# TensorE's rounds of attention work in another order, in a two-layer encoder on one core

## The reference, cut to what matters

```
proj = x @ w_in + b_in          # q_a k_a v_a g_a | q_b k_b v_b g_b | q_idx k_idx w_idx | r_a r_b
# index scores, top-k: which keys a query may see in branch B
index_score = sum_h w_idx[h] * relu(q_idx[h] . k_idx)
# branch B: softmax attention over the selected keys (8 heads, one shared key/value)
p = softmax(q_b k_b * scale + bias, selected keys only);   y_b = p v_b
# branch A: stick-breaking attention (8 heads)
z = q_a k_a * scale;  log_keep = log_sigmoid(-z) for keys before the query
later = sum of log_keep over the later keys before the query
y_a = exp(log_sigmoid(z) + later) v_a
merged = sigmoid(r_a) * ((y_a * silu(g_a)) @ w_proj_a) + sigmoid(r_b) * ((y_b * silu(g_b)) @ w_proj_b)
x = layer_norm(ALPHA * x + merged @ w_out)
```

## Time and profile before

| | us |
|---|---|
| median of 3 runs | 1096.7 (1094.59 to 1096.8) |
| the profiled execution, its own time | 1093.59 |
| its span, first to last instruction | 1091.8 |
| PE busy | 1040.2 (95%) |
| DVE busy | 566.0 (52%) |
| POOL busy | 492.9 (45%) |
| ACT busy | 474.6 (43%) |

### The profile page before, as it was taken

How to read it: one execution, slowest core, us unless ns; L and a number is a source line. 1 busy time by engine, 2 the same in 40 slices (tenths; PEclk the granted TensorE clock), 3 DMA queues, 4 the chain that set the end, 5 groups by cost and what they waited for, 6 DMA issues and landing times.

```text
span 1091.8 us, 18589 instructions
## 1 busy us (share of the span) xinstructions
PE 1040.2 (95%) x7557; PEld 921.0 (84%) x7557; DVE 566.0 (52%) x1163; ACT 474.6 (43%) x812; POOL 492.9 (45%) x334
## 2 busy tenths in 40 slices
PE   1899999998999999999999999999899999999997
PEld 1877898776889999998788599977688999999975
DVE  7438997777773111101580699877777331101137
ACT  2244335667774432223223533476777462222310
POOL 3222355453554745445434244554445474444550
PEclk9999999999999999999999999999999999999999
DMA  6621443011111223423225223321101222242322
GB/s 198 210 78 50 147 149 131 2 40 40 40 40 63 76 90 113 143 77 117 89 79 186 62 72 101 98 83 41 40 5 36 78 78 78 78 174 85 110 76 86
DMA packets 70457, 96.61 MB, mean 88 GB/s; under 512 B 4587, under 2 KB 61381, under 8 KB 69733
## 3 DMA queue, kind: packets, MB, share of 16 engines
q1 hardware_dynamic: 66068, 82.68, 23.1%
q0 software_dynamic: 3872, 11.64, 3.3%
q10 hardware_dynamic: 432, 1.11, 0.3%
HBM read 79.46 MB, written 14.78 MB: 86 GB/s over the span
## 4 chain that ended last, share of the span: by engine, by line
PE 83%; DVE 6%; ACT 3%; POOL 3%; DMA 2%; issue 2%; SPq 0%; DVEq 0%; ACTq 0%
PE ps L503 43%; PE ps L821 10%; PE ps L780 7%; PE ps L695 5%; PE ps L604 3%; PE ps L588 2%; PE ps L646 2%; PE ps L657 2%; PE ps L674 2%; DMA raw<-in_w_in 2%; POOL w_lo L1454 1%; DVE x_nat L1178 1%; PE ps L755 1%; PE ps L734 1%; PE ps L712 1%
## 5 line engine op out<-in xcount | busy, mean ns | idle before, releaser
L1454 POOL TENSOR_TENSOR w_lo<-raw,w_hi 128x1024 fp32r<-128x1024 f32 (+1 forms) x116 | 282.0, 2432 | 374.9 <-ACT w_hi L872 374.8
L503 PE MATMUL ps<-xT_hi,w_hi 128*128 128x288 f32 x960 | 284.9, 297 | 2.8 <-POOL w_lo L1454 2.8
L503 PE MATMUL ps<-xT_hi,w_lo 128*128 128x288 f32 x960 | 282.8, 295 | 0.0
L503 PE MATMUL ps<-xT_lo,w_hi 128*128 128x288 f32 x960 | 282.7, 294 | 0.0
L503 PEld LDWEIGHTS ps<-xT_hi,w_hi 128*128 128x128 f32 x960 | 180.1, 188 | 4.8 <-POOL w_lo L1454 3.4
L503 PEld LDWEIGHTS ps<-xT_lo,w_hi 128*128 128x128 f32 x960 | 180.1, 188 | 0.0
L503 PEld LDWEIGHTS ps<-xT_hi,w_lo 128*128 128x128 f32 x960 | 180.1, 188 | 0.0
L872 ACT ACTIVATE w_hi<-raw 128x1024 fp32r<-128x1024 f32 (+1 forms) x116 | 121.0, 1045 | 122.1 <-PE ps L503 72.7
L1415 DVE TENSOR_TENSOR qy<-qy,ps 128x576 f32<-128x576 f32 x32 | 24.1, 754 | 253.8 <-PE ps L503 253.8
L921 ACT ACTIVATE qy<-ps,bias 128x576 f32<-128x576 f32 x40 | 29.7, 743 | 151.6 <-PE ps L503 148.6
L1546 POOL TENSOR_TENSOR attn<-attn 128x1024 f32<-128x1024 f32 (+1 forms) x24 | 55.2, 2298 | 71.5 <-DVE attn L1350 71.5
(11 more groups left out here) (173 smaller groups left out, 2144.3 us busy)
## 6 DMA issues: line engine op xcount, KB each, us to landing
raw<-in_w_in SPq DMA_DIRECT2D x44, 1024.0 KB, 5.2
raw<-in_w_out SPq DMA_DIRECT2D x8, 1024.0 KB, 5.0
x_kept<-x_nat SPq DMA_DIRECT2D x2, 2560.0 KB, 11.6
x_nat<-x_kept SPq DMA_DIRECT2D x2, 2560.0 KB, 11.6
raw<-in_w_proj_a SPq DMA_DIRECT2D x8, 512.0 KB, 3.5
raw<-in_w_proj_b SPq DMA_DIRECT2D x8, 512.0 KB, 4.5
x_nat<-in_x_prompt SPq DMA_DIRECT2D x4, 512.0 KB, 8.5
out<-stage POOLq DMA_DIRECT2D x8, 256.0 KB, 4.9
```

The lines of the kernel that those rows point to most:

```text
L503: last = mm(out, a, b[:, HALF * half:HALF * (half + 1)], start=(k == 0 and i == 0), stop=(k == n - 1 and i == 2))
L1454: g.tensor_tensor(lo, src, hi.bitcast(f32), ALU.subtract).then_inc(s_lo, 1)
```

## The change

- Softmax: round p has L, V(p-4), T(p-2), D in place of L, T(p-2), V(p-3), D. The first two Z stand at the head of their rounds.
- Between the loops: two dense halves in place of one; the last V of softmax goes into the first round of stick-breaking.
- Stick-breaking: round p has Z(p), V(p-4), T(p-3), D in place of T(p-3), Z(p), D, V(p-3); the halves of the gates come one round earlier. In chunk 2 the sample's two products come ahead of the prompt's.
- Index scores: two pairs ahead of every 12 dense matmuls in place of one ahead of every 6.
- DVE: in softmax `yb_out` stands between the two `masked_logits`; in stick-breaking `sum_later` comes a round later, and `mask_z` waits for the transposes only ahead of its second output. ACT: one `head` moves ahead of the loop. POOL: the `rest` of a gate unit follows an earlier `log_weight`.

```diff
-HALVES_AT = {p: [p - 2] if p < NP else [2 * p - 14, 2 * p - 13] for p in range(A_LAG, NP + A_LAG)}
+HALVES_AT = {p: [p - 1] for p in range(A_LAG - 1, NP)} | {NP: [11, 12], NP + 1: [13, 14], NP + 2: [15]}
@@ dense_with_scores
-                            if k % 2 == 0:
+                            if k % 4 == 0:
                                 index_scores(s + 8 * half + k)
+                                index_scores(s + 8 * half + k + 2)
@@ stick_z: the products of c == 2 with q_s (L716) now stand ahead of the loop over A_TILES[c] (L712)
@@ PE, softmax
-                for p in range(NBP + 3):
+                for p in range(NBP + 2):
                     if p < NBP:
                         logits(p)
+                    else:
+                        stick_z(p - NBP)
+                    if p >= 4:
+                        weigh_values(p - 4)
                     if p == 2:
                         pe.wait_ge(s_trev, L * N_TR + N_TR)
-                    if 2 <= p < NBP + 2:
+                    if p >= 2:
                         transpose_probs(2 * p - 4)
                         transpose_probs(2 * p - 3)
-                    if NBP <= p < NBP + 2:
-                        stick_z(p - NBP)
-                    if p >= 3:
-                        weigh_values(p - 3)
                     if p < len(QA_GROUPS):
                         qa_group(*QA_GROUPS[p])
                 stick_z(2)
+                weigh_values(NBP - 2)
                 dense_half(0)
+                dense_half(1)
@@ PE, stick-breaking
                 for p in range(A_LAG, NP + A_LAG):
-                    stick_transpose(p - A_LAG)
                     if p < NP:
                         stick_z(p)
+                    if p == A_LAG:
+                        weigh_values(NBP - 1)
+                    else:
+                        stick_values(p - A_LAG - 1)
+                    stick_transpose(p - A_LAG)
                     for n in HALVES_AT[p]:
                         dense_half(n)
-                    stick_values(p - A_LAG)
+                stick_values(NP - 1)
@@ ACT, after log_term(2)
+                head(N_G + 2)
@@ DVE, mask_z: the wait for s_at (transposes of p - 3) now stands behind the writes of sp_slot
@@ DVE, softmax and after
-                for p in range(NBP + 4):
+                for p in range(NBP):
+                    masked_logits(2 * p)
                     if p >= 4:
                         yb_out(p - 4)
-                    if p < NBP:
-                        masked_logits(2 * p)
-                        masked_logits(2 * p + 1)
-                    if 1 <= p < NBP + 1:
+                    masked_logits(2 * p + 1)
+                    if p >= 1:
                         normalise(p - 1)
-                    (p == NBP: mask_z(0); NBP + 1: mask_z(1); NBP + 2: sum_later(0))
+                yb_out(NBP - 4)
+                normalise(NBP - 1)
+                mask_z(0)
+                yb_out(NBP - 3)
+                mask_z(1)
+                sum_later(0)
                 mask_z(2)
+                yb_out(NBP - 2)
                 sum_later(1)
                 gate_half(0)
-                sum_later(2)
                 for p in range(A_LAG, NP + A_LAG + 1):
+                    if p < NP:
+                        mask_z(p)
+                    if p == A_LAG:
+                        yb_out(NBP - 1)
+                    for n in HALVES_AT[p - 1]:
+                        gate_half(n)
                     if p > A_LAG and (p - A_LAG) % A_CHUNKS == 0:
                         ya_out((p - A_LAG) // A_CHUNKS - 1)
-                    (mask_z(p), gate_half of HALVES_AT[p], sum_later(p))
+                    if p <= NP:
+                        sum_later(p - 1)
@@ POOL, after log_weight(p)
-                    if p >= A_LAG:
-                        for n in HALVES_AT[p]:
-                            if n % 2:
-                                rest(N_G + 2 + n // 2)
-                for n in range(5, A_UNITS):
+                    for n in HALVES_AT.get(p + 1, []):
+                        if n % 2:
+                            rest(N_G + 2 + n // 2)
+                for n in range(6, A_UNITS):
                     rest(N_G + 2 + n)
```

More of the change, by code:

```diff
@@ L708, in stick_z @@
                         pe.wait_ge(s_zm, L * NP + p)
+                    if c == 2:
+                        for n in range(2):
+                            mm(ps[:, n, 256:256 + S_HALF], q_s[:, m, :, :],
+                                      kT_a[:, m, S_HALF * n:S_HALF * n + S_HALF], start=True, stop=True)
                     for i, at, nk in A_TILES[c]:
@@ L713, in stick_z @@
                                       kT_a[half, m, PAST + DEC:PAST + DEC + nk], start=True, stop=True)
[L714 to L717, removed]
                     last.then_inc(s_z, 1)
@@ L1316, in mask_z @@
                     if p >= 3:
-                        dve.wait_ge(s_at, L * NP + p - 2)
+                        dve.wait_ge(s_lw, L * NP + p - 2)
                     elif p:
                         dve.wait_ge(s_pt, L * N_B + N_B)
-                    if p >= 3:
-                        dve.wait_ge(s_lw, L * NP + p - 2)
                     n = 256 if c == 2 else 512
@@ L1335, in mask_z @@
                                            ALU.add).then_inc(s_min, 1)
+                    if p >= 3:
+                        dve.wait_ge(s_at, L * NP + p - 2)
                     if c == 2:
@@ L1371, in ya_out @@
                     v.tensor_copy(qy[:, 4 + m, DEC:TOK], ps[:, 6, :]).then_inc(s_ya, 1)
-                for p in range(NBP + 4):
+                for p in range(NBP):
+                    masked_logits(2 * p)
                     if p >= 4:
                         yb_out(p - 4)
-                    if p < NBP:
-                        masked_logits(2 * p)
-                        masked_logits(2 * p + 1)
-                    if 1 <= p < NBP + 1:
+                    masked_logits(2 * p + 1)
+                    if p >= 1:
                         normalise(p - 1)
[L1381 to L1386, removed]
+                yb_out(NBP - 4)
[4 more added lines that the diff above has]
+                sum_later(0)
                 mask_z(2)
+                yb_out(NBP - 2)
                 sum_later(1)
                 gate_half(0)
-                sum_later(2)
                 for p in range(A_LAG, NP + A_LAG + 1):
+                    if p < NP:
[4 more added lines that the diff above has]
+                        gate_half(n)
                     if p > A_LAG and (p - A_LAG) % A_CHUNKS == 0:
                         ya_out((p - A_LAG) // A_CHUNKS - 1)
-                    if p < NP:
-                        mask_z(p)
-                    if p < NP + A_LAG:
-                        for n in HALVES_AT[p]:
-                            gate_half(n)
-                    if p < NP:
-                        sum_later(p)
+                    if p <= NP:
+                        sum_later(p - 1)
                 dve.wait_ge(s_ya, L * 2 * PAIRS + 2 * PAIRS)
```

## The result

| | before | after |
|---|---|---|
| median | 1095.64 us (1093.96 to 1096.8, 4 runs) | 1070.99 us (1070.61 to 1071.31, 4 runs) |
| profiled execution, its own time | 1093.59 | 1071.31 |
| its span | 1091.8 | 1069.5 |

What follows compares the result with a forecast made beforehand. PE, busy 95% of the span, was taken as the bound. Per layer 2.4 + 3.2 + 3.7 + 1.4 + 1.2 = 11.9, twice 23.8, off 1093.6: 1069.8; plus 3.1, 1072.9, said as 1072; 8-of-10 range 1066 to 1083.

Steps and rivals of the forecast that it cites:

- softmax rounds: Softmax on PE: the new order has three tile shape changes a round, not four; 0.20 us a round, 2.4 a layer.
- index scores: Index scores on PE: joining two groups removes two shape changes of 0.20 us; 3.2 us a layer, low end 1.5.
- hole: PE's 3.46 us wait before stick-breaking's first T, and the half clock behind it, go: 3.7 us a layer, from 2.2 to 5.
- loop, shape changes and stalls: Stick-breaking rounds: one shape change fewer in rounds 4 to 11, 1.4 us a layer, and PE's late waits gone, 1.2.
- rival (c): Shape change isn't what costs, so reordering saves only the hole and the loop's stalls: 1087 us; chance 0.06.
- The 64-row rounds: Softmax rounds 14 to 17: no gain, 0.15 us charged in 16 and 17 each; free joins would add 0.8 a layer.
- Rival (e): The burst of index scores makes PE wait for relu; their saving of 6.4 us shrinks to 2: 1077; chance 0.08.
- Rival (a): The clock falls anyway, by two new waits of 1.5 and 1.0 us: 1.4 us a layer, 1075.5; chance 0.14.
- rival (b): ACT or DVE paces the new stick-breaking loop, rounds staying at 6.5 to 6.9 us: 1079; chance 0.16.
- The stalls of the series: Stick-breaking: mask, ACT and scans in series make DVE lag; scans a round later remove PE's waits, 1.2 us a layer.
- Their heads and rests follow PE and only move earlier: Long dense stages: their heads and rests were held to be off the path, with nothing charged for them.
- `yb_out` at nothing: Softmax on DVE: `yb_out` waits for the V just issued, holding DVE some 0.5 us a round; costed at nothing.

Runs made afterwards that it cites:

- x_tv: Kernel after with transposes put back ahead of the values in the softmax rounds alone: 1081.74 us, ratio 0.9886 to the kernel before.
- x_index: Kernel before with only the index scores changed, two pairs at a time: 1088.57 us, ratio 0.9945.
- b1: Kernel after with mask_z(0) ahead of yb_out(16) and normalise(19) on DVE: 1069.79 us, ratio 0.9772 to the kernel before.
- b5: b4 with POOL's rest left ahead of log_weight(0), as in the kernel after: 1066.82 us, ratio 0.9741 to the kernel before.
- x_hole_lag: Kernel before with the second dense half ahead of the stick-breaking loop, rests moved with the halves, and the scans one round later: 1082.81 us, ratio 0.9894.
- x_series: Kernel after with the scans (sum_later) back in the round of their own mask on DVE: 1109.28 us, ratio 1.0133 to the kernel before.
- x_hole: Kernel before with the second dense half ahead of the stick-breaking loop, other halves with gates, heads and rests one round earlier: 1112.06 us, ratio 1.0166.
- x_lag: Kernel before with only the scans (sum_later) one round later on DVE, PE's order untouched: 1106.28 us, ratio 1.0107.
- b3: b1 plus dense_half(0) ahead of stick_z(2) on PE and log_weight(0) ahead of rest(N_QA + 5) on POOL: 1068.77 us, ratio 0.9769 to the kernel before.
- b4: b3 with gate_half(0) ahead of sum_later(1) on DVE: 1066.86 us, ratio 0.9741 to the kernel before.

## Why the prediction was right, and where its steps were not

Per layer, us saved, each stage read from PE's starts in the first layer:

| step | predicted | measured |
|---|---|---|
| softmax rounds | 2.4 | 2.3 |
| index scores | 3.2 | 3.1 |
| hole | 3.7 | 3.6 |
| loop, shape changes and stalls | 2.6 | 2.8 |
| sum | 11.9 | 11.8 |

**Softmax.** The change of shape is what costs: the same transposes take 0.85 ahead of D and 1.03 ahead of V, in x_tv as before, and rival (c) falls. The 64-row rounds were charged rightly: six transposes of 64 rows last 0.50 ahead of D (225.31 to 225.81 in the trace after) as they did ahead of V (230.22 to 230.72 in the trace before), so no 0.8 more was won. Round 3 was charged 0.3 where it loses two changes, which is 0.4; the sum doesn't notice.

**Index scores.** The size holds twice, in the trace and in x_index. That both sides of a group cost 0.20 was the less certain half of it, and it held: the pair of groups is 0.39 shorter. Rival (e) falls.

**The hole.** From T of round 20 to the first V it was 23.2, plus 0.4 for the V that has come in; from 241.12 to 261.13 it is now 20.0. The forecast was 19.6, of whose saving of 4.0 it took 3.7. The waits of 1.5 and 1.0 came as 1.28 and 0.92, and of the 0.4 by which D2 is late 0.3 lie in the first T. Rival (a) falls: two waits of this size left the clock at 1.00. What made b1 to b5 possible was named too: `mask_z(0)` behind `yb_out(16)`.

**The loop.** It lasted 79.7 (from 269.30 to 349.02) and lasts 76.9 (261.13 to 338.01); x_hole_lag splits the 2.8 into 1.3 for the stalls and 1.5 for the shape changes, where 1.2 and 1.4 were forecast. Rounds are 6.3, and rival (b) falls, but not by its own argument: scans did stretch by 1.2 beside POOL, as it feared, and the slack of the later `sum_later` took it.

**What failed is how the terms were joined, not the terms.** Three statements of the text stand there by themselves though each hangs on another edit; the first two are wrong as they stand, though their sum was right:

- The stalls of the series were priced at 1.2 a layer, from the kernel before. That price held only with the hole in place: DVE's round of 6.88 was given a start of 4 us by it, and few rests lay beside the scans. In the new order the series costs 19 a layer (x_series), and closing the hole without cutting the series makes the kernel slower (x_hole). Both kernels also have more of their scans beside a `rest`; how much of the loss is that and how much the lost start stays open. The prediction listed 3.7 and 1.2 side by side as if each could be had without the other.
- "Their heads and rests follow PE and only move earlier" costed POOL's order at nothing. Left as it was, with the scans a round later, it costs 4.8 us a layer and a fall of the clock (x_lag); and where the rests lie beside the scans it is DVE that pays.
- `yb_out` at nothing holds only with V ahead of T; with T ahead of V it costs some 2.5 a layer (x_tv). The prediction gave this reason, the V between L and T, but not as something that its sum hung on.

**The total.** Two layers of 11.8 make 23.6, and the span fell by 22.3. The difference of 1.3 stands ahead of the changed pieces of each layer. In the first it is 0.8: the first index score starts at 70.84 where it was 70.03. In the second it is 0.5: PE waits 0.98 for `ki_nat` ahead of L567 (575.13), where it waited 0.51 (585.62). Neither comes from the change: in the other profiled executions, whatever the order, that score starts anywhere from 69.77 to 71.09, and that wait is 0.3 to 1.2.

The forecast of 1072 for the median hangs on one more step: the 3.1 us by which the median before stood above its profiled execution were added to 1069.8, which gives 1072.9, and 1072 was said. They did not carry over; the profiled execution after, 1071.31, is the slowest of its four. Against it the sum of 1069.8 was 1.5 too low, and the two errors are of opposite sign. That the forecast lies 1 us from the measured 1070.99 is in part luck; the terms, measured each by itself, are not.

## What to carry to other kernels

When an engine's stall and another engine's lag lie in the same stretch, price the removal of one with the other still there and with it gone: of the two edits here each alone makes the kernel slower, by 1.7% and 1.1%, and both together make it 1.1% faster. In both losses POOL's `rest` has a part, beside the scans in the one and too late in the other, so look also at where the work of a third engine comes to lie. A wait moved into another engine's queue is free only for the order in which it was read, so write down for each instruction that is passed what stands behind it (here `normalise` behind `yb_out`, `rest` behind `log_weight`, `gate_half` behind the scans). On TensorE, count changes of tile shape as you count instructions: two of them a group were 0.4 us, and a reordering that no other engine notices takes them away.

## What the hardware did that was not expected

- DVE's scans nearly stand still beside POOL. Two scans of 128x512 take 2.34 alone, and 3.56 in the kernel after (288.20), where a `rest` runs until 289.57: 1.2 us lost in 1.4 us side by side. Four of 384 take 2.43 alone and 4.58 in x_hole, with all 2.52 us of a `rest` inside: 2.15 lost. It can also fall on POOL: the `rest` of 3.31 started at 254.85, just as the second of two scans did, and these scans took 2.33; other rests take 2.4. Over the execution the 72 scans are busy 60.2 us before, 71.1 after, 79.9 in x_hole and 81.8 in x_series, with the same work. DVE's passes over PSUM don't stretch: 1.22 at 284.61 in the kernel after, with a `log_weight` beside it from 284.77.
- The granted clock depends on more than the wait ahead. It fell behind single waits of 3.46 (before) and 4.78 us (x_lag), and held with 1.28 and 0.92 a few microseconds apart. In x_hole it fell behind 2.23 (at 288.41), 2.57 and 2.59, and held at 1.00 behind another 2.23 (at 822.82) and behind 2.30 (at 317.82), so the length of the wait does not decide it alone. And in the profiled execution of b3 it fell where there is nothing to wait for, in the dense stage with the index scores. The windows of that stage, in the kernel after and then in b3:

```profile
110.00:126.00 16.00, 16.00 (x95) 13.10 (x95) 15.27 (x34) 6.44 (x12) 4.75 (x2) 1.00 0.25 79
```

```profile
110.00:126.00 16.00, 16.00 (x76) 13.38 (x75) 15.31 (x31) 5.73 (x11) 4.73 (x2) 0.79 0.16 49
```

PE is full in both, and b3's clock is 0.79; b3's own time, 1070.77, is some 2 us above its other runs. The same stage has 0.89 in b4's profiled execution (110 to 126) and 0.86 in x_hole_lag's (120 to 132), again with no wait. Where the times of one kernel part, the mean clock of the span does too: b1's are 1068.0 and 1068.8 at 0.998, 1070.8 and 1071.0 at 0.995. So a median of four can move by a microsecond or two with it, which is as much as b1 to b3 have to show. What brings the clock down there stays open.
